# A hybrid attention, recurrence and convolution backbone: attention tiles of 16 rows by 8 columns, keys and queries divided into parts in the projections, one bias table per head laid out in DRAM

## The chip, the cores and the metric

The kernel runs on one core of a Trainium2 chip. The metric is the device time of one execution in microseconds, the median of several runs. All numbers are float32. TensorE works on float32 values that are divided into a high part (rounded, type fp32r) and a low part (what is left), so that a product of two matrices becomes three passes: high times high, low times high, high times low. "PE" is TensorE, "DVE" VectorE, "ACT" ScalarE, "POOL" GpSimd, and "SP" the engine that issues most DMAs.

## The reference

Two layers, 1024 latent tokens (16 rows of 64), 256 context tokens, width 1024. The even layer projects to queries, keys, values, a recurrence input and its gate, does windowed attention with 8 heads of 64, and a recurrence (RG-LRU) in both directions; the odd layer is a gated short convolution. Each is followed by a SwiGLU feed-forward layer. What the change touches is the attention:

```
def neighbourhood_attention(q, k, v, k_ctx, v_ctx, rpb):
    # grid of rows x 64; a query sees 8 rows x 16 columns of keys, and all 256 context keys
    row_start = jnp.clip(jnp.arange(rows) - wr // 2, 0, rows - wr)          # wr = 8
    col_start = jnp.clip(jnp.arange(GRID_W) - WIN_COLS // 2, 0, GRID_W - WIN_COLS)   # 64, 16
    ...
        bias = rpb[:, dr[:, None, :, None], dc[None, :, None, :]]
        s_win = jnp.einsum("bqjhd,bqrjchd->bhqjrc", qb, kw) + bias[None]
        s_ctx = jnp.einsum("bqjhd,bnhd->bhqjn", qb, k_ctx)
        logits = jnp.concatenate([s_win.reshape(...), s_ctx], axis=-1)
        p = jax.nn.softmax(logits.astype(jnp.float32), axis=-1).astype(v.dtype)
        return (jnp.einsum("bhqjrc,bqrjchd->bqjhd", p_win, vw)
                + jnp.einsum("bhqjn,bnhd->bqjhd", p_ctx, v_ctx))
```

## The kernel before

Five programs, one for each engine, are written out in order by hand and meet only in semaphores; nothing is reordered. The stages follow each other on PE: the input and its norm (0 to 58 us), four projection rounds i = 0 to 3 (58 to 291 us), the values (to 348 us), attention (348 to 531 us), the output projection, and three feed-forward or convolution stages (to the end).

A projection round makes 128 columns each of the recurrence input, the query, the key and the recurrence gate: ten PE groups in the order `GROUPS`, written (unit, part), where unit 0 is the recurrence input, 1 the query, 2 the key, 3 the gate, and part 2 the context. They rotate through five PSUM banks, and ACT evacuates them in order. A weight unit of 512 KB is loaded by SP into one of two halves of `raw`, and POOL divides it with `split` into `w_hi4` and `w_lo4` (two instructions, the high part first). The groups are followed by `gates(i)`, twelve small products that need `gate_hi` (ACT), `gate_lo` (DVE), `xc_hi` (ACT, after the convolution `x_conv` on DVE) and `xc_lo` (DVE). After them ACT and DVE do the recurrence (`recur`), while PE goes on with the next round. DVE's order in `recur(i)` is: four `mod_part(i, 0..3)` (a modulation vector summed from `mod_in_p`, 512 KB each, loaded by SP), the two scans, four `mod_part(i, 4..7)`, and then `convolve(i + 1)` and `gate_low(i + 1)`. So the convolution of the next round stands behind the landing of four modulation loads.

SP's order in the loop over i = 1 to 3 is: two weight units of round i, four modulation loads (from i = 2 on), a unit, four modulation loads (from i = 2 on), a unit, then a wait for `gates(i - 1)` on PE and eight loads of gate weights. Loop i therefore begins when PE has finished `gates(i - 2)`, that is beside round i - 1.

The bias of the attention is written early to DRAM as `rpb_wide`, 64 by 64 columns for each head and row offset: a fill with a large number, one large DMA and 15 small ones (L613 to L623). ACT writes queries and keys whole to DRAM (`q_spill`, `k_spill`, L1822 and L1827). In the attention SP loads them for each head (`load_head`, L681 and L682), and POOL divides them there (`split_head`, L940 to L958).

In the attention a step s is a head and a block b of 128 queries, which is 2 rows of 64 columns. The keys of a block are whole rows: 8 rows for four blocks of the eight (512 keys) and 10 rows for the other four (640), and 256 context keys, so 768 or 896 columns. Each step has on PE `scores` (query times high and low keys), `turn_probs` (a transpose for each 128 keys) and a share of `values`; on DVE `logits` (bias added, minimum taken) and `turned_low`; on ACT `exps` and `turned_high`. Scores of step s + 1 wait for `logits` of step s (`s_min`), since there is one buffer for them. Queries are stacked: the high part in partitions 0 to 63, the low part in 64 to 127.

## Time and profile before

| | us |
|---|---|
| median of 3 runs | 2332.86 (2331.56 to 2333.79) |
| span of the profiled execution | 2330.4 |
| PE busy in the span | 2272.5 (98%) |
| DVE, POOL, ACT busy | 1511.0, 1205.4, 850.0 |

The profiled execution was not timed apart from its span; the median of the runs is 2.5 us above the span, for what lies around it. The page's part 5 names groups of instructions by line, engine and tile; "idle before" is how long the engine had stood still ahead of them, and what ended that. The attention is the only long stage in which PE, ACT and DVE are all busy for most of the time.

### The profile page before, as it was taken

To read this page: it belongs to the slowest core of one execution; us is meant where nothing else is said; L and a number is where in the kernel's file an instruction comes from. 1 tells how busy PE (TensorE), PEld (TensorE's weight loads), DVE (VectorE), ACT (ScalarE), POOL (GpSimd) and SP (SyncE) were. 2 spreads that over 40 slices of the span, in tenths; PEclk is the share of its full clock that TensorE was granted. 3 is DMA by queue.
4 is the path that set the end of the run, shared out by engine and by line. 5 is a ranking of instruction groups with operands and counts; after the bars stand their busy time and mean duration, and the time that the engine had idled before them with its cause. 6 is when DMAs were issued, how large, how long until landed. Compare 5 with 4: busy or idle time off the path is not lost.

```text
span 2330.4 us, 27734 instructions
## 1 busy us (share of the span) xinstructions
PE 2272.5 (98%) x10486; PEld 1856.0 (80%) x10486; DVE 1511.0 (65%) x1943; ACT 850.0 (36%) x1375; POOL 1205.4 (52%) x739
## 2 busy tenths in 40 slices
PE   7999999999989999999999999999999999999998
PEld 3888887877868888888888777888788888888887
DVE  5687747872586555557777887665975555555553
ACT  3544437881443323332212523232623233332112
POOL 3333327788746555556434345574455555565340
PEclk9999999999999999999999999999999999999999
DMA  9544356624323222228664122251132222243321
GB/s 318 164 140 140 140 160 150 110 60 145 82 82 98 90 84 82 82 93 288 211 206 138 47 76 73 73 176 55 41 100 82 84 84 82 82 151 107 109 78 76
DMA packets 268617, 270.22 MB, mean 116 GB/s; under 512 B 43624, under 2 KB 212292, under 8 KB 267972
## 3 DMA queue, kind: packets, MB, share of 16 engines
...
## 4 chain that ended last, share of the span: by engine, by line
PE 87%; DVE 7%; ACT 2%; issue 2%; POOL 1%; DMA 1%; SPq 0%; DVEq 0%; POOLq 0%; ACTq 0%
PE bank L1095 27%; PE bank L1097 27%; PE bank L1096 27%; PE bank L1176 1%; DVE probs L2455 1%; PE bank L1307 1%; DVE act_lo L2067 1%; PE bank L1333 1%; PE bank L1332 1%; PE bank L1294 1%; PE bank L1130 1%; ACT probs L1876 1%; DVE act_hi L2067 1%; PE bank L1295 1%; DVE x_rms L2059 0%
## 5 line engine op out<-in xcount | busy, mean ns | idle before, releaser
L1986 DVE SCALAR_TENSOR_TENSOR h<-bank,mods,h 128x512 f32<-128x512 f32 x384 | 287.5, 750 | 271.2 <-PE bank L1097 266.2
L1056 POOL TENSOR_TENSOR slot_lo<-pair_raw,slot_hi 128x512 fp32r<-128x512 f32 x112 | 170.1, 1519 | 291.8 <-ACT slot_hi L1596 291.8
L1056 POOL TENSOR_TENSOR slot_lo<-t_sum,slot_hi 128x512 fp32r<-128x512 f32 x109 | 166.5, 1548 | 148.3 <-ACT slot_hi L1596 148.3
L1056 POOL TENSOR_TENSOR slot<-pair_raw,slot 128x512 fp32r<-128x512 f32 x144 | 230.9, 1624 | 16.0 <-ACT slot L1596 16.0
L2147 DVE TENSOR_TENSOR bank<-bank,p 128x512 f32<-128x512 f32 x53 | 37.0, 698 | 285.9 <-PE bank L1097 285.8
L1596 ACT CAST slot_hi<-pair_raw 128x512 fp32r<-128x512 f32 x112 | 69.0, 616 | 298.8 <-DMA pair_raw<-in_ffn_w_gu 234.8
L1095 PE MATMUL bank<-act_lo,slot_hi 128*128 128x512 f32 x436 | 170.8, 392 | 6.5 <-DVE act_lo L2067 5.9
L1095 PE MATMUL bank<-a,slot_hi 128*128 128x512 f32 x436 | 171.5, 393 | 2.3 <-ACT p L1605 0.8
L1097 PE MATMUL bank<-a,slot_hi 128*128 128x512 f32 x436 | 170.5, 391 | 0.0
L1097 PE MATMUL bank<-act_lo,slot_hi 128*128 128x512 f32 x436 | 170.2, 390 | 0.0
L1096 PE MATMUL bank<-act_lo,slot_lo 128*128 128x512 f32 x436 | 170.0, 390 | 0.0
L1096 PE MATMUL bank<-a,slot_lo 128*128 128x512 f32 x436 | 169.7, 389 | 0.0
L1096 PE MATMUL bank<-act_hi,w_lo 128*128 128x512 f32 x376 | 148.3, 394 | 0.0
L1095 PE MATMUL bank<-act_hi,w_hi 128*128 128x512 f32 x368 | 145.3, 395 | 2.7 <-DVE proj_lo L2321 2.7
L1067 POOL TENSOR_TENSOR act_lo<-low_f,act_lo 128x512 fp32r<-128x512 f32 x80 | 102.3, 1318 | 87.5 <-ACT act_lo L1636 87.5
L1096 PE MATMUL bank<-act_hi,slot 128*128 128x512 f32 x364 | 141.9, 390 | 0.0
L1097 PE MATMUL bank<-act_hi,slot 128*128 128x512 f32 x364 | 141.8, 390 | 0.0
L1095 PE MATMUL bank<-act_hi,slot 128*128 128x512 f32 x364 | 141.7, 389 | 0.0
L1095 PE MATMUL bank<-act_lo 128*128 128x512 f32 x320 | 125.8, 393 | 0.0
L1097 PE MATMUL bank<-act_lo 128*128 128x512 f32 x320 | 125.1, 391 | 0.0
L1596 ACT CAST slot_hi<-t_sum 128x512 fp32r<-128x512 f32 x109 | 67.7, 622 | 156.2 <-PE bank L1097 92.7
L1096 PE MATMUL bank<-act_lo 128*128 128x512 f32 x320 | 124.6, 389 | 0.0
...
## 6 DMA issues: line engine op xcount, KB each, us to landing
pair_raw<-in_ffn_w_gu SPq DMA_DIRECT2D x88, 512.0 KB, 4.6
mod_in_f<-in_mod_w SPq DMA_DIRECT2D x48, 512.0 KB, 4.0
...
mod_in_p<-in_mod_w SPq DMA_DIRECT2D x32, 512.0 KB, 6.1
pair_raw<-in_o_w_in SPq DMA_DIRECT2D x24, 512.0 KB, 3.8
raw<-in_e_w_in SPq DMA_DIRECT2D x20, 512.0 KB, 5.0
...
a_f<-z_spill SPq DMA_DIRECT2D x18, 512.0 KB, 6.1
```

What stands on the lines that cost most here:

```text
L1056: nc.gpsimd.tensor_tensor(low, from_, high, ALU.subtract).then_inc(s_wlo, 1)
L1067: nc.gpsimd.tensor_tensor(lo, full, hi, ALU.subtract).then_inc(s_l2, 1)
L1095: pe.matmul(dst, w_hi, x_hi, start=first, stop=False)
L1096: pe.matmul(dst, w_lo, x_hi, start=False, stop=False)
L1097: return pe.matmul(dst, w_hi, x_lo, start=False, stop=last)
L1130: mm = pe.matmul(bank[:, b, m:m + 1], acc[:, m * P:(m + 1) * P], ones[:, 0:1], start=True, stop=True)
L1176: mm = pe.matmul(bank[0:2, 4 + 2 * c + a, :], cond[:, k, :], mod_ring[:, u % 8, a * HALF:(a + 1) * HALF], start=(k == 0), stop=(k == FT - 1))
L1294: pe.matmul(out_, q, kh[:, src:src + n], start=True, stop=False)
L1596: nc.scalar.copy(slot(st, n, p)[0], from_).then_inc(s_whi, 1)
L1986: V.scalar_tensor_tensor(out=dst, in0=bank[:, b, :], scalar=mods[:, gate, m:m + 1], in1=dst, op0=ALU.mult, op1=ALU.add).then_inc(s_hup, 1)
L2067: V.tensor_tensor(lo, LOW_F[n][k], hi, ALU.subtract).then_inc(s_ld, 1)
L2147: V.tensor_tensor(to, bank[:, x_bank(p), :], p1_at(p), ALU.add).then_inc(s_made, 1)
```

## The change

1. A block of queries is now all 16 rows of 8 columns, and a tile of keys the same shape. A block sees its own tile and its two neighbours: 256 window keys at the two edges and 384 elsewhere, so 512 or 640 columns with the context.
2. ACT writes each query or key group from PSUM into `qk_raw` in the new order (a "piece", five in a round). POOL divides it there (`split_piece`), and ACT stores the high and the low part to DRAM (`store_piece`). In the attention, SP loads high and low parts straight into the operands, and `split_head` is gone.
3. The bias is one table of 896 columns per head and query, `rpb_full`, made by SP in three steps: `fill_bias` (8 DMAs, 3.67 MB), `widen_bias` (56 DMAs of 120 runs of 32 bytes into `rpb_cols`), and `place_bias`, twice (56 DMAs each, DRAM to DRAM, of 64 runs of 256 bytes).
4. POOL also makes the high part of the attention's output (`y_ready`), which ACT made before; ACT and DVE write the output in the new order, and the first two output products take three quarters of the attention's part before they wait for the last.
5. The values are stored by token and loaded with 9 DMAs for a pair of heads in place of 1.

```
-        q_spill = nc.dram_tensor("q_spill", (LT, P, SEQ), F32, kind="Internal").ap()
-        k_spill = nc.dram_tensor("k_spill", (LT, P, KEYS), F32, kind="Internal").ap()
-        v_spill = nc.dram_tensor("v_spill", (P, TT + CT, LT * P), F32, kind="Internal").ap()
+        q_spill = nc.dram_tensor("q_spill", (2, LT, P, SEQ), F32, kind="Internal").ap()
+        k_spill = nc.dram_tensor("k_spill", (2, LT, P, KEYS), F32, kind="Internal").ap()
+        v_spill = nc.dram_tensor("v_spill", (KEYS, LT * P), F32, kind="Internal").ap()
         r_spill = nc.dram_tensor("r_spill", (LT, P, SEQ), F32, kind="Internal").ap()
         z_spill = nc.dram_tensor("z_spill", (HID // P, P, SEQ), F32, kind="Internal").ap()
-        rpb_wide = nc.dram_tensor("rpb_wide", (HEADS, NR, GRID, GRID), F32, kind="Internal").ap()
-
-
-        k_raw = at(16, "k_raw", [P, KEYS])
-        q_raw = at(21, "q_raw", [P, SEQ])
+        COLS = 8
+        ROWS = SEQ // GRID
+        KINDS = ((0, 2 * COLS), (GRID - 2 * COLS, 2 * COLS), (None, 3 * COLS))
+        KIND_AT = (0, 2 * P, 4 * P)
+        KIND_ALL = 7 * P
+        rpb_cols = [nc.dram_tensor(f"rpb_cols{j}", (HEADS, COLS, w // COLS, NR * COLS), F32, kind="Internal").ap() for j, (_, w) in enumerate(KINDS)]
+        rpb_full = nc.dram_tensor("rpb_full", (HEADS, P, KIND_ALL), F32, kind="Internal").ap()
...
+        def key_tiles(b):
+
+            return [t for t in (b - 1, b, b + 1) if 0 <= t < TT]
...
-            sp.wait_ge(s_far, 1)
-            wide = rpb_wide.rearrange("h r c k -> (h r c k)").rearrange("(n p w) -> n p w", n=4, p=P)
-            for n in range(4):
-                sp.dma_start(wide[n], far_rows[:, :]).then_inc(s_filled, 16)
-
-
-
-            sp.wait_ge(s_filled, 64)
-            sp.wait_ge(s_neg, 1)
-            inner = bass.AP(tensor=rpb_wide.tensor, offset=8 * GRID, ap=[[GRID * GRID, HEADS * NR], [GRID + 1, GRID - 15], [1, 16]])
-            sp.dma_start(inner, rpb_neg[:, 7:23].rearrange("p (a k) -> p a k", a=1).to_broadcast([HEADS * NR, GRID - 15, 16])).then_inc(s_wide, 16)
-            for c in (*range(8), *range(GRID - 7, GRID)):
-                k = min(max(c - 8, 0), GRID - 16)
-                sp.dma_start(rpb_wide[:, :, c, k:k + 16].rearrange("h r k -> (h r) k"), rpb_neg[:, k - c + 15:k - c + 31]).then_inc(s_wide, 16)
+            def fill_bias():
+
+                sp.wait_ge(s_far, 1)
+                far = far_rows[:, :].rearrange("p (a k) -> p a k", a=1).to_broadcast([P, 4, KIND_ALL // 4])
+                for hd in range(HEADS):
+                    sp.dma_start(rpb_full[hd].rearrange("p (a k) -> p a k", a=4), far).then_inc(s_filled, 16)
+
+            def widen_bias():
+
+                sp.wait_ge(s_neg, 2)
+                for j, c, tile, src in WIDENED:
+                    from_ = rpb_mid if j == 2 else rpb_neg
+                    sp.dma_start(rpb_cols[j][:, c, tile, :].rearrange("h (r k) -> h r k", k=COLS), from_[:, src:src + COLS]).then_inc(s_wide, 16)
+
+            def place_bias(rows):
+
+                sp.wait_ge(s_filled, 16 * HEADS)
+                sp.wait_ge(s_wide, 16 * len(WIDENED))
+                for row in rows:
+                    lo = row_start(row)
+                    for j, (_, w) in enumerate(KINDS):
+                        for tile in range(w // COLS):
+                            at_ = KIND_AT[j] + tile * P + lo * COLS
+                            sp.dma_start(rpb_full[:, row * COLS:row * COLS + COLS, at_:at_ + 8 * COLS],
+                                         rpb_cols[j][:, :, tile, (lo - row + 7) * COLS:(lo - row + 15) * COLS]).then_inc(s_full, 16)
...
+            fill_bias()
             for i in range(1, LT):
                 for j in range(2):
                     load_unit(4 * i + j, j, column_unit(w_in, i * P + order_p[j]))
+                if i == 1:
+                    widen_bias()
+                else:
+                    place_bias(range(ROWS // 2 * (i - 2), ROWS // 2 * (i - 1)))
...
+                kh, kl, qs = (tile.bitcast(F32) for tile in head_tiles(head))
                 for a in range(2):
                     half = slice(64 * a, 64 * a + 64)
-                    sp.dma_start(k_to[half, :], k_spill[pair, 64 * hh:64 * hh + 64, :]).then_inc(s_hraw, 16)
-                    sp.dma_start(q_to[half, :], q_spill[pair, 64 * hh:64 * hh + 64, :]).then_inc(s_hraw, 16)
+                    sp.dma_start(kh[half, :], k_spill[0, pair, own, :]).then_inc(s_head[head % 2], 16)
+                    sp.dma_start(qs[half, :], q_spill[a, pair, own, :]).then_inc(s_head[head % 2], 16)
+                    sp.dma_start(kl[half, :], k_spill[1, pair, own, :]).then_inc(s_head[head % 2], 16)
...
+            def split_piece(i, x):
+
+                n, g = 5 * i + x, PIECES[x]
+                w = CTX if GROUPS[g][1] == 2 else HALF
+                pool.wait_ge(s_projev, 10 * i + 5 + g + 1)
+                if n >= 2:
+                    pool.wait_ge(s_qh[n % 2], X_DONE + 16 * (n // 2))
+                nc.gpsimd.tensor_tensor(qk_hi[:, n % 2, 0:w], qk_raw[:, n % 3, 0:w], ones[:, 0:1].to_broadcast([P, w]),
+                                        ALU.mult).then_inc(s_qkh, 1)
+                pool.wait_ge(s_qkh, n + 1)
+                nc.gpsimd.tensor_tensor(qk_raw[:, n % 3, 0:w].bitcast(F32R), qk_raw[:, n % 3, 0:w], qk_hi[:, n % 2, 0:w], ALU.subtract).then_inc(s_qkl, 1)
+
+            for i in range(LT):
+                split_piece(i, 0)
+                split_piece(i, 1)
+                if i + 1 < LT:
+                    split(4 * i + 4, 0, 0, used_p(i, 0))
+                    split(4 * i + 5, 1, 1, used_p(i, 1))
+                else:
+                    for j in range(2):
+                        split(U_V + j, j, j, used_p(i, j))
+                for x in (2, 3, 4):
+                    split_piece(i, x)
+                if i >= 1:
+                    store_lru(i - 1)
+                for j in (2, 3):
+                    split(4 * i + 4 + j if i + 1 < LT else U_V + j, j, j % 2, used_p(i, j))
...
+            def y_ready(g):
+
                 pool.wait_ge(s_fold, g + 1)
                 pool.wait_ge(s_invr, g + 1)
-                y = y_f[block_of(g)]
-                nc.gpsimd.tensor_tensor(y, y, inv_rows[block_of(g)[0], :], ALU.mult).then_inc(s_yf, 1)
+                y, rows = block_of(g, y_f), rows_of(g)[0]
+                one_row = ones[rows, 0:32].rearrange("p (a c) -> p a c", a=1).to_broadcast([64, ROWS, 32])
+                nc.gpsimd.tensor_tensor(y, y, inv_rows[rows, :].rearrange("p (r c) -> p r c", c=32), ALU.mult).then_inc(s_yf, 1)
                 pool.wait_ge(s_yf, g + 1)
-
-            def y_low(g):
+                nc.gpsimd.tensor_tensor(block_of(g, act_hi), y, one_row, ALU.mult).then_inc(s_yh, 1)
                 pool.wait_ge(s_yh, g + 1)
-                nc.gpsimd.tensor_tensor(act_lo[block_of(g)], y_f[block_of(g)], act_hi[block_of(g)], ALU.subtract).then_inc(s_yl, 1)
+                nc.gpsimd.tensor_tensor(block_of(g, act_lo), y, block_of(g, act_hi), ALU.subtract).then_inc(s_yl, 1)
...
             out_weight(0)
-            lru_low(0)
-            y_scaled(BLOCKS - 4)
-            lru_low(1)
-            y_low(BLOCKS - 4)
-            lru_low(2)
-            y_scaled(BLOCKS - 3)
-            lru_low(3)
-            y_low(BLOCKS - 3)
+            for j in range(2):
+                lru_low(j)
+            y_ready(BLOCKS - 4)
             out_weight(1)
-            y_scaled(BLOCKS - 2)
-            y_low(BLOCKS - 2)
-            out_weight_low(1)
-            y_scaled(BLOCKS - 1)
-            y_low(BLOCKS - 1)
+            y_ready(BLOCKS - 3)
+            for j in range(2, LT):
+                lru_low(j)
+            for g in range(BLOCKS - 2, BLOCKS):
...
+                q, n = qs[:, b * P:(b + 1) * P], width(s)
+                k0 = CTX + P * key_tiles(b)[0]
+                for out_, part in ((bank_f[:, HALF - n:HALF], slice(k0, k0 + n)), (bank_f[:, HALF:HALF + CTX], slice(0, CTX))):
+                    pe.matmul(out_, q, kh[:, part], start=True, stop=False)
+                    mm = pe.matmul(out_, q, kl[:, part], start=False, stop=True)
                 mm.then_inc(s_sc, 1)
...
-                    project_out(0, 0, bank[:, 0, :], range(LT, FT))
-
-
-            project_out(0, 1, bank[:, 1, :], range(LT, FT))
+                    project_out(0, 0, bank[:, 0, :], (*range(LT, FT), *range(LT - 1)))
...
+                def store_piece(i, x):
+
+                    n, (unit, part) = 5 * i + x, GROUPS[PIECES[x]]
+                    w = CTX if part == 2 else HALF
+                    act.wait_ge(s_qkl, n + 1)
+                    for a, (tile, done) in enumerate(((qk_hi[:, n % 2, 0:w].bitcast(F32), s_qh[n % 2]), (qk_raw[:, n % 3, 0:w], s_ql[n % 3]))):
+                        if part < 2:
+                            dst = q_spill[a, i] if unit == 1 else k_spill[a, i, :, CTX:]
+                            act.dma_start(dst.rearrange("p (j h n) -> h p j n", j=TT, h=2)[part],
+                                          tile.rearrange("p (j n) -> p j n", j=TT)).then_inc(done, 16)
+                        else:
+                            act.dma_start(k_spill[a, i, :, 0:CTX], tile).then_inc(done, 16)
...
+                    piece = PIECES.index(g)
+                    n = 5 * i + piece
+                    if n >= 3:
+                        act.wait_ge(s_ql[n % 3], X_DONE + 16 * (n // 3))
+                    if part < 2:
+                        nc.scalar.activation(by_blocks(qk_raw[:, n % 3, :]), by_rows(bank[:, g % 5, :]), ACT.Copy,
+                                             scale=-(64 ** -0.5) if unit == 1 else 1.0).then_inc(s_projev, 1)
+                    else:
+                        nc.scalar.copy(qk_raw[:, n % 3, 0:w], bank[:, g % 5, 0:w]).then_inc(s_projev, 1)
+                    if piece:
+                        store_piece(i, piece - 1)
...
+                at0 = KIND_AT[kind(b)] + CTX * kind(b)
+                V.tensor_tensor_reduce(out=probs[s % 3][:, 0:w + CTX], in0=bank_f[:, HALF - w:HALF + CTX],
+                                       in1=bias_t[:, hd % 2, at0:at0 + w + CTX], scale=1.0, scalar=FAR, op0=ALU.add, op1=ALU.min,
                                        accum_out=low_all[:, s:s + 1]).then_inc(s_min, 1)
```

On POOL, at the change from round 0 to round 1 of the projections, the order before was two halves of each weight unit (`w_hi`, `w_lo`), one unit after the other:

```order
L916 MEMSET gate_w 128x512
L918 MEMSET x_pad 128x2
L918 MEMSET x_pad 128x3
L918 MEMSET x_pad 128x1
L900 TENSOR_TENSOR w_hi<-raw,ones 128x1024
L903 TENSOR_TENSOR w_lo<-raw,w_hi 128x1024
L900 TENSOR_TENSOR w_hi<-raw,ones 128x1024
L903 TENSOR_TENSOR w_lo<-raw,w_hi 128x1024
```

The same place after:

```order
L959 MEMSET x_pad 128x1
L967 TENSOR_TENSOR qk_hi<-qk_raw,ones 128x512
L970 TENSOR_TENSOR qk_raw<-qk_raw,qk_hi 128x512
L967 TENSOR_TENSOR qk_hi<-qk_raw,ones 128x512
L970 TENSOR_TENSOR qk_raw<-qk_raw,qk_hi 128x512
L940 TENSOR_TENSOR w_hi<-raw,ones 128x1024
L943 TENSOR_TENSOR w_lo<-raw,w_hi 128x1024
L940 TENSOR_TENSOR w_hi<-raw,ones 128x1024
L943 TENSOR_TENSOR w_lo<-raw,w_hi 128x1024
L967 TENSOR_TENSOR qk_hi<-qk_raw,ones 128x512
L970 TENSOR_TENSOR qk_raw<-qk_raw,qk_hi 128x512
```

Two pieces now stand ahead of two weight units of the next round, and three pieces behind them.

On ACT, in round 0 from the fourth query or key group (piece 3 in the new kernel) to the gates' operands, before:

```order
L1822 ACTIVATE qk_out<-bank 128x512 [waits proj_done]
L1827 DMA k_spill<-qk_out 128x512 [waits proj_evacuated]
L1822 ACTIVATE qk_out<-bank 128x512 [waits proj_done]
L1827 DMA k_spill<-qk_out 128x512 [waits proj_evacuated]
L1822 ACTIVATE qk_out<-bank 128x256 [waits proj_done]
L1827 DMA k_spill<-qk_out 128x256 [waits proj_evacuated]
L1833 CAST gate_hi<-gate_w 128x512 [waits gate_w_landed,bias_filled,h_spilled]
```

The same place after, where `qk_piece_lo` is POOL's signal that a piece is divided:

```order
L1852 ACTIVATE qk_raw<-bank 128x8x8x8 [waits x_landed2_then_qk_lo_stored0,proj_done]
L1834 DMA k_spill<-qk_hi 128x8x64 [waits qk_piece_lo]
L1834 DMA k_spill<-qk_raw 128x8x64
L1855 COPY qk_raw<-bank 128x256 [waits x_landed3_then_qk_lo_stored1,proj_done]
L1834 DMA k_spill<-qk_hi 128x8x64 [waits qk_piece_lo]
L1834 DMA k_spill<-qk_raw 128x8x64
L1861 CAST gate_hi<-gate_w 128x512 [waits gate_w_landed,h_spilled]
```

ACT's cast to `gate_hi` now stands behind the stores of pieces 2 and 3, which wait for POOL.

On SP, from the gate weights of round 0 (L657, before L630) to the modulation loads of the loop i = 2 (L664, before L637), before:

```order
L630 DMA gate_w<-in_e_lru_wi 64x64 x2
L637 DMA mod_in_p<-in_mod_w 128x1024 x4
L566 DMA raw<-in_e_w_in 128x8x128 x4
L630 DMA gate_w<-in_e_lru_wr 64x64 x2
L630 DMA gate_w<-in_e_lru_wi 64x64 x2
L630 DMA gate_w<-in_e_lru_wr 64x64 x2
L630 DMA gate_w<-in_e_lru_wi 64x64 x2
L566 DMA raw<-in_e_w_in 128x8x128 x2
L637 DMA mod_in_p<-in_mod_w 128x1024 x4
```

The same place after:

```order
L664 DMA mod_in_p<-in_mod_w 128x1024 x4
L631 DMA rpb_full<-far_rows 512x1x224 x8
L582 DMA raw<-in_e_w_in 128x8x128 x2
L638 DMA rpb_cols<-rpb_neg 8x15x8 x32
L638 DMA rpb_cols<-rpb_mid 8x15x8 x24
L582 DMA raw<-in_e_w_in 128x8x128 x2
L657 DMA gate_w<-in_e_lru_wr 64x64 x2
L657 DMA gate_w<-in_e_lru_wi 64x64 x2
L657 DMA gate_w<-in_e_lru_wr 64x64 x2
L657 DMA gate_w<-in_e_lru_wi 64x64 x2
L582 DMA raw<-in_e_w_in 128x8x128 x2
L649 DMA rpb_full<-rpb_cols 8x8x64 x56
```

The fill now stands ahead of the weights of round 1, and 56 DMAs of `place_bias` ahead of the modulation loads; the loop i = 3 has the same 56 at the same place.

## Rows read from the trace of the kernel before

**Rows 1.** The page: span, and busy time of each engine with its share and instructions.

```profile
span 2330.4 us, 27734 instructions
PE 2272.5 (98%) x10486; PEld 1856.0 (80%) x10486; DVE 1511.0 (65%) x1943; ACT 850.0 (36%) x1375; POOL 1205.4 (52%) x739
```

**Rows 2.** Windows: stretch, length, busy PE, PEld, DVE, ACT, POOL, clock, DMA share, GB/s.

```profile
58.00:348.00 290.00, 289.62 (x1408) 243.29 (x1408) 204.37 (x185) 127.25 (x172) 93.87 (x49) 0.99 0.47 150
348.00:524.00 176.00, 162.43 (x1033) 137.38 (x1034) 140.33 (x269) 146.06 (x241) 139.52 (x77) 1.00 0.52 106
```

**Rows 3.** Timeline of PE in the attention: start, us, operation.

```profile
370.06 0.34 PE L1332 MATMUL bank<-pt_hi,v_even 128*128 128x384 f32 x1
370.24 0.34 PE L1333 MATMUL bank<-pt_lo,v_even 128*128 128x384 f32 x1
...
371.12 0.82 PE L1307 MATMUL bank<-ident,probs 128*128 128x128 f32 x6
371.69 0.37 PE L1332 MATMUL bank<-pt_hi,v_even 128*128 128x256 f32 x1
```

**Rows 4.** Groups by form, 366 to 520 us: busy, mean ns, idle before.

```profile
L2455 DVE CUSTOM_DVE_ANT_0 probs<-bank,bias_t 128x896 f32<-128x896 f32 x28 | 30.5, 1089 | 14.9 <-PE bank L1295 14.8
L2468 DVE TENSOR_TENSOR pt_lo<-bank,pt_hi 128x896 fp32r<-128x896 f32 x28 | 30.3, 1081 | 0.4 <-ACT pt_hi L1889 0.4
L1876 ACT ACTIVATE probs<-probs,low_all 128x896 f32<-128x896 f32 x28 | 29.3, 1046 | 10.0 <-DVE low_all L2455 9.3
L979 POOL TENSOR_TENSOR y_f<-y_f,inv_rows 64x512 f32<-64x512 f32 x14 | 18.0, 1284 | 19.7 <-DVE y_f L2474 12.5 <-PE bank L1295 6.3
L2455 DVE CUSTOM_DVE_ANT_0 probs<-bank,bias_t,low_ctx 128x512 f32<-128x512 f32 x21 | 15.8, 751 | 0.7
```

**Rows 5.** One line of the kernel: duration ns min/median/max, first and last start, form.

```profile
L903 POOL TENSOR_TENSOR w_lo<-raw,w_hi x20: 2339/2428/3267, 33.0 to 284.4; 128x1024 fp32r<-128x1024 f32 x20
```

**Rows 6.** Timeline of PE after a wait of 3.6 us.

```profile
534.51 0.80 PE L1095 MATMUL bank<-act_hi,o_hi 128*128 128x512 f32 x1 [3.59 <-POOL w_lo L1011]
535.10 0.63 PE L1096 MATMUL bank<-act_hi,w_lo 128*128 128x512 f32 x1
```

**Rows 7.** Timelines of POOL, ACT, DVE and PE at the end of round 0.

```profile
97.64 1.90 POOL L900 TENSOR_TENSOR w_hi<-raw,ones 128x1024 fp32r<-128x1024 f32 x1 [17.93 <-DMA raw<-in_e_w_in]
100.45 1.26 ACT L1835 CAST xc_hi<-x_conv 128x1280 fp32r<-128x1280 f32 x1
104.52 3.41 DVE L2416 TENSOR_TENSOR xc_lo<-x_conv,xc_hi 128x1024 fp32r<-128x1024 f32 x1
109.79 0.28 PE L1095 MATMUL bank<-xc_hi,gate_hi 128*128 128x256 f32 x1
```

**Rows 8.** A window in which the DMA engines are full, columns as in rows 2.

```profile
92.00:96.00 4.00, 4.00 (x19) 3.34 (x18) 1.42 (x2) 0.00 (x0) 0.00 (x0) 1.00 1.08 357
```

**Rows 9.** Timeline of SP's issues; then two lines' issue ns, min/median/max.

```profile
117.00 1.53 SPq L630 DMA_DIRECT2D gate_w<-in_e_lru_wr  x2
...
123.96 2.55 SPq L637 DMA_DIRECT2D mod_in_p<-in_mod_w  x4
...
433.27 5.88 SPq L672 DMA_DIRECT2D bias_t<-rpb_wide  x4
...
L630 SPq DMA_DIRECT2D gate_w<-in_e_lru_wi x16: 467/597/603, 80.9 to 237.5; - x16
...
L623 SPq DMA_DIRECT2D rpb_wide<-rpb_neg x15: 407/411/17398, 52.9 to 76.2; - x15
```

**Rows 10.** Timelines beside round 1: DVE's sums, DVE's last gate operand, PE's gates.

```profile
141.76 12.46 DVE L2378 SCALAR_TENSOR_TENSOR mod_acc_p<-mod_in_p,cond,mod_acc_p 128x1024 f32<-128x1024 f32 x4
...
163.06 3.42 DVE L2416 TENSOR_TENSOR xc_lo<-x_conv,xc_hi 128x1024 fp32r<-128x1024 f32 x1
...
167.79 0.36 PE L1095 MATMUL bank<-xc_hi,gate_hi 128*128 128x256 f32 x1
```

**Rows 11.** DMA issues: count, KB each, median us to landing.

```profile
mod_in_p<-in_mod_w SPq DMA_DIRECT2D x32, 512.0 KB, 6.1
```

311 lines of the change are left out of this document (127 added, 184 removed).

## The prediction

> **What bounds the kernel now.** I read the page first: PE is busy for 98% of the span [rows 1], so what matters is PE's work and what makes PE wait. The windows by stage separate two kinds of stretch [rows 2]. From 58 to 348 us (projections and values) PE is busy for 289.6 of 290 us: nothing is spare, and whatever makes PE wait adds to the time. From 348 to 524 us (attention) PE's busy time is 162 of 176 us, and DVE, ACT and POOL are busy for 140, 146 and 140. That stretch has 66 turns of the loop (64 steps and two of lead), 2.67 us each. Behind it the change touches only the first output products, and 1785 us follow that I leave as they are.
>
> **The attention gets shorter on PE.** In the timeline the start after 384 columns comes 0.18 us later, 0.46 ns for a column, and six transposes take 0.57 us, 0.095 each [rows 3]. Before, a step has on average 832 columns of scores in two passes (0.76 us), 6.5 transposes (0.62), a quarter of 6656 value columns (0.76) and a quarter of four small transposes (0.10): 2.24 us. After, it has 608 columns (0.56), 4.75 transposes (0.45), a quarter of 4864 value columns (0.56) and 0.10: 1.67 us.
>
> DVE's pass takes 1.089 us for 896 columns and 0.751 for 512, 0.88 ns a column; its second pass (1.081) and ACT's exponential (1.046) are as long for 896 [rows 4]. I give all four passes this slope. 224 columns less, twice a step, take 0.39 us from each. From the busy time for a turn [rows 2] DVE goes from 2.13 to about 1.6 us (its separate pass over the context goes as well) and ACT from 2.21 to 1.7 (an output cast for each four steps goes to POOL). POOL loses the division of queries and keys. So PE, DVE and ACT all come to 1.6 to 1.7 us. The loop also has a chain: scores wait for the pass of the step before. After, that is 0.56 for scores, about 0.15 until they are written, 0.85 for the pass on 640 columns and some 0.2 of signals: 1.8 us. Before, the real turn stood 0.43 us (a factor of 1.19) above PE's own work. The same factor gives 2.0 us, the same difference 2.1, the chain 1.8. I take 2.1, with bounds of 1.85 (chain) and 2.4 (no better than half the gain). 66 turns save 66 x 0.57 = 38 us. From that go 2.5 us at the start: the first values are loaded by nine issues behind six of head 1, 15 at 0.6 us, then 3 us of landing and four POOL passes over 640 columns (1.6 us each, from 2.43 for 1024 and a gap), 19 us after 348, while PE wants them after eight turns, 17 us. At the end POOL is late. `y_ready` is three passes, of which the first has 1.28 us [rows 4], 3.7 in all; a weight unit is 1.90 [rows 7] and 2.43 us [rows 5], a low part of the recurrence has the second's shape, 2.4. From `y_ready(11)` to the last `lru_low` POOL has 3 x 3.7 + 2 x 4.3 + 4 x 2.4 = 29.3 us, and PE reaches the first output product after 11.3 turns, 23.7 us. PE waits 5.6 us there, and gets back 2 of the 3.6 us that it waits now a little later [rows 6]. Attention and its end: -38 + 2.5 + 3.6 = **-32 us** (bounds -48 and -12).
>
> **Round 0 of the projections gets longer.** ACT now stores piece 2 before it evacuates group 7 and casts `gate_hi`, and it waits for POOL's division of piece 2. On POOL that stands behind two weight units of round 1. Their first was waited for until 97.64 us already [rows 7]. On SP's queue 3.67 MB of fill now stand before them. The DMA engines are full there and move 357 GB/s [rows 8], so the units land 10.3 us later, or 10.8 with their own stores; I take 108.4. POOL then needs 2 x 4.37 us for the two units and 2.3 for the piece (half of 4.3, and gaps): 119.5. ACT issues two stores, evacuates, waits for piece 3, issues two more: `gate_hi` starts at 122.6, and `xc_hi` is done at 125.0 in place of 101.7 [rows 7]. DVE's `xc_lo` then takes 1.6 us where POOL is idle, or the 6.2 it takes now (104.52 + 3.41 - 101.7), since POOL is reading: 126.7 to 131.2, in the middle 129. PE's first gate product, now at 109.79, starts about 19 us later. After a wait PE is slow at first: behind the one of 3.6 us two matmuls start 0.59 us apart where 512 columns usually take 0.23 [rows 6, 3]; I put 2 us on each long wait. **+21 us** (15 if the fill takes 8 us and DVE is free, 30 if the queue moves small runs more slowly).
>
> **Rounds 1 and 2: modulation loads behind 56 placing DMAs.** SP begins this part when PE ends a round's gates (117.00) and issues eight gate loads and two units until 123.96, then at once four modulation loads [rows 9]. DVE uses them from 141.76, and because POOL works beside it the four sums last until 154.2, 37.4 us after the gates' end at 116.8 [rows 10]. The new kernel puts 56 DMAs between. No row shows a DMA from DRAM to DRAM. The nearest is a gate weight load, also 64 runs of 256 bytes: 597 ns, 0.63 with the gap [rows 9]; the small bias writes have 411 ns, 0.45 with it. From below it is 56 x 0.45 = 25 us, from above a bias load with the queue full (runs of 256 bytes too, four in 5.88 us, 1.47 each), 82 us. I take 0.63: 35.3 us. Then the last modulation load is issued 7.0 + 35.3 + 2.5 = 44.8 us after the gates and lands 5.5 to 6.1 us later [rows 11], and DVE ends its last sum 1.3 us behind that, at 51.9 in place of 37.4: 14.5 us late. The convolution, `xc_hi` and `xc_lo` follow; `xc_lo` ends at 166.5 now and PE wants it at 167.8 [rows 10], so 1.3 us are spare. PE waits 13 us and 2 for the slow start, **+15 us**, in round 1 and again in round 2: +30 (bounds 6 and 125). `widen_bias`, 56 x 0.45 = 25 us of SP in round 0, is hidden: unit 6 behind it is wanted only in the middle of round 1.
>
> **Round 3 and the rest.** There is no placing before round 3. Five pieces cost POOL about 10 us; some of it meets DVE's passes over two SBUF operands, which take 3.4 us beside POOL. DVE is 6 us later against 1.3 spare: **+5 us** (2 to 8). The order of elements that ACT, DVE and POOL write in costs nothing in my sum (no row has it; from 0 to 0.1 us for each of 100 passes, off PE's path). The larger stores of ACT, 10 issues of 0.35 to 0.6 us in a round, lie in its waits for PE.
>
> **Sum.** -32 + 21 + 30 + 5 = +24 us on the span of 2330.4, and 2.5 around it, by which the median of 2332.86 stands above that span: **2357 us**.
>
> **Rivals.**
> (a) The stalls are shallow, and it gets faster. If a placing DMA costs 0.45 us, the 56 take 25 us, DVE is 4 us late and PE 3 in each of two rounds. With 15 in round 0 and 3 in round 3 that makes +24, against -(66 x 0.77 - 6) = -45 at 1.9 us a turn: 2312 us. It needs both. For it speaks that 0.45 us is measured for 15 DMAs of small runs; the turning point with the attention at -32 is 0.45 us a DMA and 20 us in round 0. Chance 0.24.
> (b) Placing is slower than any issue: DRAM to DRAM copies of 256 bytes hold the queue at 1.0 us each. 56 us in place of 35 add 21 twice: 2399 us; at the upper bound of 1.47, 47 us twice, 2451. For it speaks that the bias loads with runs of 256 bytes hold SP for that long [rows 9]. Chance 0.12. The Trainium skill, "DMA: Bandwidth & Descriptors", section "Specifications", gives 512 bytes as the least size for full rate and says that smaller ones are read, modified and written; it gives no time for it. No row here tells a run of 32 or 256 bytes apart by such a rule.
> (c) The attention keeps the distance between engines that it has: 2.4 us a turn, -18 + 6 = -12 us: 2377 us. For it: three engines of equal load and one score buffer. Against it: POOL, whose outputs ACT waits for now, gets 1 us a turn less. Chance 0.14.
> (d) The forecast, 2340 to 2375. Chance 0.50.
>
> The measurement tells 0.2%, some 5 us, from no change. Faster than that is (a) without its edge: 0.22. Within it lies what is between (a) and the forecast: 0.07. Slower: 0.71. The range reaches from (a) to (b): 2312 to 2398; the likeliest case's own is 2340 to 2375.
>
> **What would show it.** PE waits at three places between 110 and 300 us: before the first gate product of round 0 (about 19 us, behind DVE's `xc_lo`, and ACT's stores of piece 2 waiting for POOL), and in rounds 1 and 2 before the sums `mod_acc_p` (10 to 13 us each, behind DVE, which waits for `mod_in_p`). SP's issues at the placing line are 0.6 us apart. 66 turns of attention last about 140 us. Wrong would be: no wait of DVE for `mod_in_p`; fill and weights landing by 100 us; or a turn under 1.8 or over 2.4 us.

## The result, and the profile after

The changed kernel takes 2410.91 us (median of 4 runs, 2409.97 to 2413.76) against 2333.32 (2331.56 to 2335.60) on the same chip: a ratio of 1.0337 with a 95% interval of 1.0324 to 1.0349. It is slower, as forecast, but by 77.6 us where 24 were forecast, and outside the range of 2312 to 2398. The page: span, busy time of the engines, the chain of work by engine, then its lines.

```profile
span 2408.7 us, 27503 instructions
PE 2250.9 (93%) x10278; PEld 1839.3 (76%) x10278; DVE 1478.5 (61%) x1895; ACT 817.0 (34%) x1359; POOL 1209.8 (50%) x764
PE 73%; DVE 10%; SPq 7%; POOL 3%; issue 3%; ACT 2%; DMA 2%; DVEq 0%; POOLq 0%; ACTq 0%
PE bank L1115 23%; PE bank L1117 23%; PE bank L1116 23%; SPq L649 3%; SPq L638 2%; DVE x_conv L2396 1%; PE bank L1196 1%; DVE act_lo L2097 1%; DVE act_hi L2097 1%; PE bank L1324 1%; ACT probs L1910 1%; SPq L631 1%; DVE mod_acc_p L2408 1%; DMA mod_in_p<-in_mod_w 1%; DVE probs L2476 1%
```

PE has 22 us less to do than before [rows 1] and 98% has become 93%. On the chain stands SP's queue, with the placing (L649), the widening (L638) and the fill (L631): 7% of the span on an engine that computes nothing. Next, PE's first gate product of each round, the modulation totals (L1150), and the first scores: start, us, and in brackets PE's idle time before it.

```profile
129.69 0.55 PE L1115 MATMUL bank<-xc_hi,gate_hi 128*128 128x256 f32 x1 [19.46 <-issue]
...
214.65 3.55 PE L1150 MATMUL bank<-ones,mod_acc_p 128*128 128x1 f32 x16 [25.83 <-DVE mod_acc_p L2408]
230.88 0.55 PE L1115 MATMUL bank<-xc_hi,gate_hi 128*128 128x256 f32 x1 [12.68 <-issue]
...
295.18 3.54 PE L1150 MATMUL bank<-ones,mod_acc_p 128*128 128x1 f32 x16 [6.18 <-DVE mod_acc_p L2408]
311.34 0.55 PE L1115 MATMUL bank<-xc_hi,gate_hi 128*128 128x256 f32 x1 [12.62 <-issue]
...
374.33 0.55 PE L1115 MATMUL bank<-xc_hi,gate_hi 128*128 128x256 f32 x1 [2.51 <-issue]
...
440.34 0.39 PE L1309 MATMUL bank<-k_hi,q_st 128*128 128x256 f32 x1 [0.68 <-ACT v_tok L1901]
```

Set against the same products before (the first two are in [rows 7, 10], the other three here), they tell where the time went, and which terms of the sum were wrong. The six distances add up to 78.3 us, the difference of the two spans.

```profile
225.82 0.36 PE L1095 MATMUL bank<-xc_hi,gate_hi 128*128 128x256 f32 x1
...
283.87 0.36 PE L1095 MATMUL bank<-xc_hi,gate_hi 128*128 128x256 f32 x1
...
348.29 0.50 PE L1294 MATMUL bank<-k_hi,q_st 128*128 128x512 f32 x1 [0.68 <-ACT v_tok L1867]
```

| from the product before to this one | before | changed | added | forecast |
|---|---|---|---|---|
| start to gates, round 0 | 109.8 | 129.7 | +19.9 | +21 |
| gates 0 to gates 1 | 58.0 | 101.2 | +43.2 | +15 |
| gates 1 to gates 2 | 58.0 | 80.5 | +22.4 | +15 |
| gates 2 to gates 3 | 58.1 | 63.0 | +4.9 | +5 |
| gates 3 to first scores | 64.4 | 66.0 | +1.6 | 0 |
| first scores to the end | 1982.1 | 1968.4 | -13.7 | -32 |

SP's queue in the changed kernel: start, time that the group took to issue, line, tiles, count.

```profile
86.86 14.15 SPq L631 DMA_DIRECT2D rpb_full<-far_rows  x8
...
106.49 25.61 SPq L638 DMA_DIRECT2D rpb_cols<-rpb_neg  x32
132.14 16.98 SPq L638 DMA_DIRECT2D rpb_cols<-rpb_mid  x24
...
161.05 6.21 SPq L582 DMA_DIRECT2D raw<-in_e_w_in  x2
167.39 37.76 SPq L649 DMA_DIRECT2D rpb_full<-rpb_cols  x56
205.19 1.87 SPq L664 DMA_DIRECT2D mod_in_p<-in_mod_w  x4
...
246.14 37.41 SPq L649 DMA_DIRECT2D rpb_full<-rpb_cols  x56
283.60 1.95 SPq L664 DMA_DIRECT2D mod_in_p<-in_mod_w  x4
```

And DVE at the two places where it had waited for the loads:

```profile
208.98 4.07 DVE L2408 SCALAR_TENSOR_TENSOR mod_acc_p<-mod_in_p,cond,mod_acc_p 128x1024 f32<-128x1024 f32 x3 [35.83 <-DMA mod_in_p<-in_mod_w]
...
289.57 5.46 DVE L2408 SCALAR_TENSOR_TENSOR mod_acc_p<-mod_in_p,cond,mod_acc_p 128x1024 f32<-128x1024 f32 x4 [21.72 <-DMA mod_in_p<-in_mod_w]
294.94 2.71 DVE L2394 TENSOR_SCALAR x_conv<-x_pad,par 128x256 f32<-128x256 f32 x2
297.69 10.66 DVE L2396 SCALAR_TENSOR_TENSOR x_conv<-x_pad,par,x_conv 128x256 f32<-128x256 f32 x6
```

The mechanism is the one forecast: widening or placing on SP, the modulation loads behind it, DVE's sums behind these, then the convolution, then PE. A placing block takes 37.4 to 37.8 us (35.3 forecast). The widening takes 42.6 us (25 forecast, "hidden"). It is not hidden: SP leaves it at 149, then stands 10.6 us at the units of round 2 for POOL's `w_lo`, and the placing starts at 167.39, 21.0 us later than the forecast had it (7.0 us after the gates' end, which came at 139.4).

After each of these waits PE is also slow for some microseconds. The sixteen modulation products and then the windows (columns as in [rows 2]) show it: the products before, to be set against the 3.55 us above, and the granted clock behind the wait of 19.46 us, 0.50 first (the lower level of 1.2 GHz) and then 1.00 (2.4 GHz).

```profile
166.09 1.84 PE L1130 MATMUL bank<-ones,mod_acc_p 128*128 128x1 f32 x16
```

```profile
130.00:132.00 2.00, 2.00 (x7) 1.71 (x7) 0.00 (x0) 0.88 (x3) 0.00 (x0) 0.50 0.17 24
...
136.00:138.00 2.00, 2.00 (x14) 1.66 (x13) 1.22 (x1) 1.93 (x4) 0.00 (x0) 1.00 0.10 6
```

The twelve gate products take 7.0 to 7.1 us in every round before (109.79 to 116.81 in round 0), and 9.7, 8.7, 9.4 and 8.6 us in rounds 0 to 3 of the changed kernel. Waits and slow products together are nearly the whole of the table: 25.8 + 12.7 + 1.7 + 2.7 = 42.9 of the 43.2 us, 6.2 + 12.6 + 1.7 + 1.6 = 22.1 of the 22.4, and 2.5 + 2.3 of the 4.9. (The slow gate products of a round fall into the distance to the next round.)

In the attention the forecast turn is there. ACT's exponentials of steps 4, 8, 12, 16 and 48, then PE's waits at the first values and at the end:

```profile
450.00 0.83 ACT L1910 ACTIVATE probs<-probs,low_all 128x640 f32<-128x640 f32 x1 [0.38 <-DVE low_all L2476]
...
468.34 0.72 ACT L1910 ACTIVATE probs<-probs,low_all 128x512 f32<-128x512 f32 x1 [10.68 <-DVE low_all L2476]
...
480.43 0.83 ACT L1910 ACTIVATE probs<-probs,low_all 128x640 f32<-128x640 f32 x1
...
488.52 0.72 ACT L1910 ACTIVATE probs<-probs,low_all 128x512 f32<-128x512 f32 x1
...
557.05 0.73 ACT L1910 ACTIVATE probs<-probs,low_all 128x512 f32<-128x512 f32 x1
```

```profile
464.53 0.76 PE L1349 MATMUL bank<-pt_hi,v_even 128*128 128x512 f32 x1 [8.63 <-POOL v_odd L1006]
...
601.63 0.79 PE L1115 MATMUL bank<-act_hi,o_hi 128*128 128x512 f32 x1 [6.60 <-POOL act_lo L1026]
...
621.69 0.47 PE L1115 MATMUL bank<-act_hi,w_hi 128*128 128x512 f32 x1 [2.77 <-POOL w_lo L1040]
```

From step 16 to 48, 32 turns take 68.5 us, 2.14 each (2.1 forecast). The eight turns from step 4 to 12 take 30.4 us: 13.3 us more than at 2.14, where 2.5 were forecast for the first values. At the end POOL costs waits of 10.1 us (the two of 6.6 and 2.8 us and one of 0.7 between them), against 3.6 before [rows 6].

### The profile page after: what moved, and what is told of

Its sections match the earlier page's. It is cut to its first block, busy times and chain, and to the rows that moved or that the text cites. A ratio compares the mean times of both kernels' runs of the same rounds, so it can differ in the third digit from the quotient of the medians.

```text
span 2408.7 us, 27503 instructions
## 1 busy us (share of the span) xinstructions
PE 2250.9 (93%) x10278; PEld 1839.3 (76%) x10278; DVE 1478.5 (61%) x1895; ACT 817.0 (34%) x1359; POOL 1209.8 (50%) x764
## 4 chain that ended last, share of the span: by engine, by line
PE 73%; DVE 10%; SPq 7%; POOL 3%; issue 3%; ACT 2%; DMA 2%; DVEq 0%; POOLq 0%; ACTq 0%
PE bank L1115 23%; PE bank L1117 23%; PE bank L1116 23%; SPq L649 3%; SPq L638 2%; DVE x_conv L2396 1%; PE bank L1196 1%; DVE act_lo L2097 1%; DVE act_hi L2097 1%; PE bank L1324 1%; ACT probs L1910 1%; SPq L631 1%; DVE mod_acc_p L2408 1%; DMA mod_in_p<-in_mod_w 1%; DVE probs L2476 1%
```

## The experiments

Each kernel is the changed one with the edit shown; times are medians beside runs of the kernel before on the same chip, ratios go against that kernel.

**1. Modulation loads ahead of the placing.**

```
                 if i >= 2:
                     for k in range(4, FT): load_mod_p(i - 2, k)      # was behind place_bias
                 if i == 1: widen_bias()
                 else: place_bias(...)
```

> Edit: before rounds 2 and 3 SP issues the modulation loads (k = 4 to 7) ahead of the 56 placing DMAs instead of behind them. Nothing is left out. Theory A (place in SP's queue): PE's waits before the sums (25.8 and 6.2 us) and the gate waits behind them (12.7 and 12.6) come from DVE's wait for mod_in_p alone. Then DVE's last sum of round 1 ends near 179 us, the convolution near 191, the first gate product is at about 194 us instead of 230.9, and round 2 loses about 18 us in the same way; units 10 and 14, now behind the placing, still come in time. 2411 - 55 = 2356 us (2350 to 2365). Rival B (DMA traffic of 256-byte copies slows whatever is in flight): the modulation loads still land late, beside the copies: 2395 us or more. Rival C (ACT and POOL, busy with the pieces, hold the gates back in every round): the waits before the sums go, those before the gates stay: 2411 - 32 = 2379 us.

2369.2 us (ratio 1.0160, 1.0144 to 1.0175): 41.7 us of the 77.6 are the place in the queue. PE waits nowhere for `mod_acc_p` any more. Theory A holds for these waits, but its 55 us are not reached, and the time lies outside its range, between A and rival C: the first gate product of round 1 comes at 199.59, not 194, and that of round 2 66.8 us later, not 58. The waits before the gates, which A had go too, stay at 9.8 and 7.1 us (12.7 and 12.6 before the edit), and that of round 3 grows from 2.5 to 6.1. DVE has its loads, but beside a busy POOL the last four sums of round 1 take 11.3 us (12.5 before, [rows 10]) and the convolution 12.3, where it took 6.3 in the kernel before.

```profile
199.59 0.55 PE L1115 MATMUL bank<-xc_hi,gate_hi 128*128 128x256 f32 x1 [9.84 <-issue]
```

**2. Weight units 4 and 5 ahead of the fill** (`fill_bias()` moved behind the two `load_unit` of round 1).

> Edit: weight units 4 and 5 are issued ahead of the eight fill DMAs. Nothing is left out. Theory A: the units land near 98 us as in the kernel before, POOL is through piece 2 ten us earlier, and the first gate product of round 0 comes at about 119 us instead of 129.7. But SP reaches the widening DMAs no earlier (it only swaps two blocks), so the modulation loads are issued at 205 us as now and the gates of round 1 start at 231 as now: the ten us are waited for in round 1 instead. 2411 us (2406 to 2413). Rival: each round's lateness adds to the next, since rounds follow each other on PE: 2400 us.

2408.9 us (1.0325, 1.0308 to 1.0342): the time is the expected one, a gain that is nowhere in it. The way there was not quite the expected one. The wait of round 0 goes from 19.46 to 6.55 us, and the first gate product comes 14.9 us earlier:

```profile
114.78 0.55 PE L1115 MATMUL bank<-xc_hi,gate_hi 128*128 128x256 f32 x1 [6.55 <-issue]
...
207.32 3.54 PE L1150 MATMUL bank<-ones,mod_acc_p 128*128 128x1 f32 x16 [24.82 <-DVE mod_acc_p L2408]
223.59 0.55 PE L1115 MATMUL bank<-xc_hi,gate_hi 128*128 128x256 f32 x1 [12.72 <-issue]
```

By round 1 half of it is gone: a new wait of 6.2 us for POOL's `w_lo` stands at 155.00, SP ends the widening only 2.5 us earlier, and its placing starts at 159.76, 7.6 us earlier and not at the same time as was expected. In the profiles the gates of rounds 1, 2 and 3 come 7.3, 6.0 and 6.0 us earlier, the first output product 2.8 and the end 1.3; why the attention and what follows take that back is open. That the cause of round 0's term (the fill ahead of the units) was right is shown by its own wait, not by the total.

**3. Widening and placing left out.**

> Left out: the 56 widening and 112 placing DMAs, so the bias table holds only the far value. The fill, the pieces on POOL and ACT, and the attention stay. Theory A: rounds 1 and 2 lose both stalls, round 0 keeps its 20 us and round 3 its 5: 2411 - 43 - 22 + 5 to 10 = 2354 us (2348 to 2362), and attention (scores' start to end of run) lasts as long as in the changed kernel. Rival C (pieces on ACT and POOL): PE still waits 12 us before the gates of rounds 1 and 2: 2380 us.

2361.5 us (1.0130, 1.0115 to 1.0145): the 168 DMAs cost 49.5 us. The waits before the gates of rounds 1 and 2 are under 3 us, so rival C with its 12 us falls. But the distances from gates to gates are 63.6, 62.7 and 63.6 us, and 58.0 in the kernel before: some 5 us stay in each of the three rounds, also where no DMA is added. The forecast had such a term for round 3 alone. A wait of 22.9 us stays in round 0, and 9.2 us at the first values.

**4. The same table with 40 DMAs.**

```
-        rpb_cols = [... (HEADS, COLS, w // COLS, NR * COLS) for each kind]   rpb_full (HEADS, P, KIND_ALL)
+        rpb_cols = ... (COLS, 7, HEADS, NR * COLS)                           rpb_full (P, 7, HEADS, P)
+                    sp.dma_start(rpb_full[row * COLS:row * COLS + COLS, :, :, lo * COLS:lo * COLS + 8 * COLS].rearrange("c t h n -> (c t h) n"),
+                                 rpb_cols.rearrange("c t h n -> (c t h) n")[:, (lo - row + 7) * COLS:(lo - row + 15) * COLS])
```

> Edit: the same table with 24 widening DMAs in place of 56 (all tiles of a column in one) and 16 placing DMAs in place of 112 (one for a row, 448 runs of 256 bytes each in place of 64), by another order of the table's dimensions in DRAM. Nothing is left out; the bytes and runs are the same. Theory A1 (SP pays per DMA, about 0.63 us): widening 15 us, placing 8 x 0.63 = 5 us before each of rounds 2 and 3; the stalls of rounds 1 and 2 go as without these DMAs: 2355 us, within 4 us of the kernel that leaves them out. Theory A2 (SP pays per run of bytes, so that 448 runs cost seven times 64): the placing stays at 35 us a round and the widening at 40: 2405 to 2412 us.

2361.4 us (1.0127, 1.0112 to 1.0142): the same as without the DMAs. (The bias loads of the attention change their order of elements with the table; from the first scores to the first output product it is 161.2 us, 161.3 in the changed kernel.) The widening takes SP 14.9 us, and the placing of a round, its first line here, 6.1. Behind it, nanoseconds for one issue of widening and placing:

```profile
149.91 6.12 SPq L648 DMA_DIRECT2D rpb_full<-rpb_cols  x8
```

```profile
L639 SPq DMA_DIRECT2D rpb_cols<-rpb_neg x16: 443/447/3279, 106.3 to 116.4; - x16
...
L648 SPq DMA_DIRECT2D rpb_full<-rpb_cols x16: 621/686/991, 149.9 to 217.3; - x16
```

In the changed kernel the two lines read:

```profile
L638 SPq DMA_DIRECT2D rpb_cols<-rpb_neg x32: 630/631/3302, 106.5 to 131.5; - x32
...
L649 SPq DMA_DIRECT2D rpb_full<-rpb_cols x112: 608/609/865, 167.4 to 282.9; - x112
```

448 runs of 256 bytes take SP 686 ns, 64 take 609. A1 is right: SP pays by the DMA.

**5. Widening alone merged.**

> Edit: the changed kernel, with only the widening merged (24 DMAs for 56); the 112 placing DMAs, their order and the modulation loads behind them stay. Nothing is left out. It measures the share of the widening in the 43 us of round 1. Theory A (widening is not hidden: SP comes out of it at 149 us and reaches the placing at 167 in place of about 150): the placing starts at about 150 us, the modulation loads are issued at 188 instead of 205, the gates of round 1 start at about 214 instead of 230.9, and the distance from round 1 to round 2 stays at 80 us: 2411 - 17 = 2394 us (2388 to 2400). Rival, the step as it was predicted (widening is hidden in round 0, and the excess of round 1 is DVE's and POOL's): 2408 to 2412 us.

2397.5 us (1.0277, 1.0259 to 1.0294).

```profile
149.44 38.10 SPq L650 DMA_DIRECT2D rpb_full<-rpb_cols  x56
187.59 2.45 SPq L665 DMA_DIRECT2D mod_in_p<-in_mod_w  x4
```

The placing starts at 149.44, 6.7 us after the gates' end at 142.8, and the loads are issued at 187.59, as theory A had it. From gates 0 to gates 1 it is 83.6 us in place of 101.2 (133.27 to 216.85), so 17.6 of the 43.2 us of round 1 are the widening's. The total gains 13.4 only, because the first gate product of round 0 comes 3.6 us later. The trace shows two parts of that: ACT's cast to `gate_hi` starts 1.9 us later (128.10 for 126.22), since the stores of piece 3 ahead of it take 3.2 us to issue in place of 1.1; and DVE's last `xc_lo` takes 2.92 us in place of 1.22, since unit 6, no longer late behind the widening, is being divided on POOL from 129.99.

```profile
130.25 2.92 DVE L2447 TENSOR_TENSOR xc_lo<-x_conv,xc_hi 128x1024 fp32r<-128x1024 f32 x1
```

From gates 1 to gates 2 it stays 80.1.

**6. Merged DMAs, and units 4 and 5 ahead of the fill.**

> Edit: the merged bias DMAs (24 widening, 16 placing) and in addition weight units 4 and 5 ahead of the eight fills. Nothing is left out. Theory A (in round 0 ACT's store of piece 2 waits for POOL, and POOL for the two units behind the fill): PE's wait before the first gate product goes from 23 us to the 6.6 us that it had where only the units were moved; now that SP is no longer late in rounds 1 and 2 the gain is kept to the end: 2361 - 17 = 2344 us (2340 to 2349). Rival: as where only the units were moved, a later wait takes the gain: 2358 us or more.

2349.1 us (1.0069, 1.0054 to 1.0085), 12.3 us less than in experiment 4: the edit that gave nothing in experiment 2 gives most of its 17 us once SP is not late behind it, though not all: 2349.1 is at the edge of theory A's range. The first gate product comes 15.9 us earlier than in experiment 4 (117.33), in round 1 still 12.2 us earlier (184.45).

**7. ACT's stores behind the casts.**

```
-                    if piece:                      +                    if piece in (1, 2):
                         store_piece(i, piece - 1)
+                # behind gate_hi and xc_hi: store_piece(i, 2); store_piece(i, 3)
```

> Edit: as the kernel before it in this call, and ACT stores pieces 2 and 3 behind the casts gate_hi and xc_hi instead of ahead of them, in all rounds. Nothing is left out. Theory A: the gates no longer wait for POOL's pieces; the waits before the first gate product (6.6 us in round 0, about 3, 3 and 6 in the others) fall to DVE's convolution alone: 2344 - 8 = 2336 us (2331 to 2341). Rival: the later stores hold POOL's pieces 3 and 4 and so the weight units 6 and 7 of the next round, and PE waits for these: 2345 to 2355 us.

2356.0 us (1.0094, 1.0079 to 1.0110): 7 us slower than experiment 6, so the rival. Round 0 gains 5.2 us and by round 2 nothing is left. In round 3 POOL waits for a store before its last piece and starts the units of the values 7 us later: this kernel's POOL, then that of experiment 6 at the same place.

```profile
310.30 0.61 POOL L966 TENSOR_TENSOR qk_hi<-qk_raw,ones 128x256 fp32r<-128x256 f32 x1 [7.72 <-DMA k_spill<-qk_hi]
...
316.12 1.88 POOL L939 TENSOR_TENSOR w_hi<-raw,ones 128x1024 fp32r<-128x1024 f32 x1 [3.85 <-DMA r_spill<-lru_q]
```

```profile
309.08 2.94 POOL L939 TENSOR_TENSOR w_hi<-raw,ones 128x1024 fp32r<-128x1024 f32 x1 [2.64 <-DMA r_spill<-lru_q]
```

**8. Attention: first values first, POOL's end spread** (`load_values(0)` ahead of `load_head(1)`; `lru_high` and `lru_low` one at a time from step 44 on; with the merged DMAs).

> Edit: the merged bias DMAs, and in the attention (1) the values of heads 0 and 1 are loaded ahead of the queries and keys of head 1, (2) the four high and low parts of the recurrence's output are taken one at a time from 20 steps before the end, instead of together at its end. Nothing is left out. Theory A: the attention's steady turn is 2.0 us; what it lost against the forecast is the wait for the first values (8.7 us, with slow turns behind it) and POOL's queue at the end (6.6, 0.7 and 2.8 us of PE waits). (1) gives 4 us, (2) gives 8: 2361 - 12 = 2349 us (2345 to 2354). Rival (engines are evenly loaded, so that moved work costs the steps that it is moved into as much): 2358 to 2362 us.

2345.5 us (1.0054, 1.0039 to 1.0069), 15.8 us less than experiment 4 (12 expected). The wait for the first values is 1.6 us where it was 8.7, with 1.4 for head 1's keys, and that of 6.6 at the end is gone; those of 0.7 and 2.8 stay. Some 3 of the 15.8 us come ahead of the first scores (388.9 against 392.1 in the profiles) and are not the edit's. The rival falls: POOL and ACT had room for the moved work.

**9. All of these together.**

> Edit: all of these together: merged bias DMAs, units 4 and 5 ahead of the fill, ACT's stores behind the casts, the values first, the recurrence's parts spread. Nothing is left out. Theory A: the places follow one another on PE, which bounds the kernel, so that the gains add: 2361 - 17 - 8 - 12 = 2324 us (2318 to 2330), under the kernel before. Rival: 2335 us or more, if one gain is taken back by a later wait.

2338.2 us (1.0021, 1.0011 to 1.0031): the rival's side, since the order of experiment 7 is in it.

**10. The same without the move of ACT's stores.**

> Edit: merged bias DMAs, units 4 and 5 ahead of the fill, the values of heads 0 and 1 first, the recurrence's parts spread; ACT's stores stay where the changed kernel has them. Nothing is left out. Theory A: without the move of ACT's stores, which gave 5 us in round 0 and lost 12 behind it, the gains of the units (12 us) and of the attention (16 us) add: 2361 - 12 - 16 = 2333 us (2329 to 2337), within 0.2% of the kernel before. Rival: a gain is taken back by a later wait: 2340 us or more.

2332.7 us (0.9996, 0.9987 to 1.0005), as expected: level with the kernel before.

**11. In addition ACT writes the high parts of queries and keys.**

```
-                nc.gpsimd.tensor_tensor(qk_hi[:, n % 2, 0:w], qk_raw[:, n % 3, 0:w], ones..., ALU.mult)      (POOL)
+                    for dst, done in ((qk_hi[:, n % 2, :], s_qkh), (qk_raw[:, n % 3, :], s_projev)):         (ACT, from PSUM)
```

> Edit: as the kernel ahead of it in this call, and the high parts of the queries and keys are written by ACT from PSUM (a second evacuation of 0.6 us for each piece) instead of by POOL; POOL keeps the low parts. Nothing is left out. Theory A (what still costs PE in the rounds is DVE, whose passes over SBUF take up to twice as long while POOL works, and POOL's pieces are the work that was added): POOL has half of the pieces' work less, 5 us a round and up to 10 where both run; the waits before the gates (7.9, 6.6, 2.9 and 2.9 us) go down by about half in the rounds 1 to 3 and by 1 to 2 us in round 0: 2333 - 8 = 2325 us (2320 to 2329), under the kernel before. Rival (ACT's chain of evacuation, stores and casts is what the gates wait for, and 3 us are added to it in each round): 2335 to 2345 us.

2321.0 us (0.9950, 0.9936 to 0.9963), 11.7 us less than experiment 10 (8 expected), and the waits before the gates go from 6.6, 2.9 and 2.3 us to 3.6, 0 and 0 in rounds 1 to 3; that of round 0 does not fall (7.4 to 8.7). The gates of round 2 and the convolution ahead of them, in experiment 10 and then here:

```profile
234.06 2.89 DVE L2395 TENSOR_SCALAR x_conv<-x_pad,par 128x256 f32<-128x256 f32 x2
236.99 7.51 DVE L2397 SCALAR_TENSOR_TENSOR x_conv<-x_pad,par,x_conv 128x256 f32<-128x256 f32 x6
```

```profile
229.12 2.10 DVE L2394 TENSOR_SCALAR x_conv<-x_pad,par 128x256 f32<-128x256 f32 x2
231.25 5.47 DVE L2396 SCALAR_TENSOR_TENSOR x_conv<-x_pad,par,x_conv 128x256 f32<-128x256 f32 x6
```

```profile
247.49 0.50 PE L1116 MATMUL bank<-xc_hi,gate_hi 128*128 128x256 f32 x1 [2.85 <-issue]
```

```profile
239.91 0.36 PE L1112 MATMUL bank<-xc_hi,gate_hi 128*128 128x256 f32 x1
```

No wait is left before the gates of rounds 2 and 3, which are 58.1 us apart again (239.91 and 297.97). The same eight passes of the convolution end 10.4 us after their start with the pieces whole on POOL and 7.6 us with half of them. The Trainium skill says in "SBUF — State Buffer", section "SBUF: two separate sides", that POOL and a DVE pass with two SBUF inputs take one pair of ports in turn, each for a whole instruction. The trace agrees: four sums take 5.46 us where POOL is idle (289.57 above), and 12.42 beside it in experiment 10 (from 221.72) and 12.46 in the kernel before [rows 10]: 3.1 each, near the 1.36 of a sum and the 1.89 of one of POOL's instructions taken in turn.

**12. In addition POOL's output part between the values.**

> Edit: as the kernel ahead of it, and POOL takes the output part that is due (groups 0, 4 and 8) between the high and the low parts of a pair's values, instead of behind both. Nothing is left out. Theory A (PE's waits of 1.8 us for ACT's probs at the second, third and fourth pair come from ACT, which waits for POOL's y_f behind 6.3 us of values): they go, 2325 - 5 = 2320 us (2316 to 2324). Rival: the loop catches up with such waits within its next turns, or the values come late in their place: no change within 2 us.

2318.3 us (0.9936, 0.9924 to 0.9949), 2.7 us less than experiment 11 where 5 were expected; the ranges of the runs touch (2316.82 to 2319.60, and 2319.64 to 2322.13). PE's waits for `probs` fall from 11.3 to 8.8 us: those at the second and third pair go, that at the fourth grows from 1.8 to 2.6. In the profiles the attention up to the first output product is only 0.6 us shorter (147.4 for 148.0), so that the 2.7 us come from this edit's mechanism is not shown. This version beats the kernel before by 0.6%, and the changed one by 3.8%.

## Why the prediction was wrong

The direction, the places and the chain of each wait were right. The sizes of round 1, round 2, the first values and the attention's end were not, and all on the same side. Two terms that came out right did so in part by luck.

- Round 0, +21: the first gate product came 19.9 us later for about 19 forecast, and the slow start took 2.7 for 2. The fill ahead of the units is the cause: with the units first its wait falls by 13 us (experiment 2), and by 15 with the merged DMAs (6). But two errors cancel in it. POOL got the units at 111.8, not 108.4, and `gate_hi` started at 126.2, not 122.6; against that `xc_lo` took 1.6 us and not the middle of 1.6 and 6.2, because the widening kept unit 6 away from POOL. Where it did not (experiment 5), the first gate product came at 133.3.
- Round 1, +15: it was 43.2, and the step that failed is "`widen_bias`, 56 x 0.45 = 25 us of SP in round 0, is hidden: unit 6 behind it is wanted only in the middle of round 1". It looked at who wants unit 6, and not at the rest of SP's queue. The issue took 0.63 us, not 0.45, and with stalls 42.6 us in all. SP then reached the placing 21.0 us late, and DVE's last sum ended at 214.5, 23.2 us behind the 191.3 of the forecast (51.9 us after the gates' end at 139.4). Experiment 5 gives 17.6 us of round 1 to the widening; the 25.6 that are left are near round 2's 22.4.
- Round 2, +15: it was 22.4. The price of placing was right (0.67 us with the gap, 0.63 forecast). What was missed stands behind the loads: the sum ended 55.5 us after the gates' end (51.9 forecast), since four loads issued within 2 us land almost together and four sums of 1.36 us follow, not one. And the convolution takes 13.4 us, where the forecast left it as it was before (6.3 us in round 1, 9.9 in round 2): the units that the placing had also held up are divided on POOL at that moment (from 295.06 to 307.27).
- Round 3, +5: it was 4.9, but only 2.5 us of it are the wait that was forecast. The other 2.3 are slow products behind the wait of round 2, which the forecast had counted in that round. That the pieces cost some 5 us a round was right in size (experiment 3); they do so in every round, and with half of them taken from POOL rounds 2 and 3 are 60.5 and 58.1 us long (experiment 11).
- Attention, -32: it was -13.7. The turn was right: 66 turns of 2.14 us are 141.3 in place of 176.1, a gain of 34.8 where 38 were forecast. The term for the first values failed: 13.3 us in place of 2.5. Its loads start 4.1 us after the first scores, because SP waits for the last value to be stored, and POOL has divided them 24 us after the first scores (19 forecast), while PE stands from 15.6 us on (17 forecast). After this wait of 8.6 us the loop had POOL's second pair of values in its way as well. POOL's end was mis-sized too. The wait at the first output product was near the forecast (6.6 us for 5.6), but none of the 3.6 us of waits a little later came back (they are 3.5 now, 2 were to go), and with what follows the end costs 7.7 us, 3.6 forecast.
- Rival (b), a placing DMA of 1.0 us, would have given 2399 and was nearest by number, but for a reason that did not hold: it took 0.67. Rival (a) needed 0.45 us for it. Rival (c)'s turn of 2.4 us was not there (2.14).

The slow start was put at 2 us for each long wait. Measured on the same products it is 2.7 us in round 0, 1.7 + 1.6 in round 1, 1.7 + 2.3 in round 2 and 1.6 behind the 2.5 us wait of round 3 (the 1.6 of the table's fifth row): 11.6 us in all, where 6 were counted.

What the change wanted is worth having: with its own stalls taken out, and POOL's pieces halved, the shorter attention puts the kernel ahead of the one before (experiments 11 and 12).
